# Filler products in TensorE's pauses, small products placed between weight blocks, and VectorE's norm chains through PSUM banks

## The reference, cut to what matters

```python
h = rms_norm(x, g);  z = h @ w_in                       # state-space branch, 8 heads, gates
x = x + rms_norm(merged @ w_mix_out, g)                 # norms 0 to 2
h = rms_norm(x, g)                                      # norm 3
x = x + rms_norm(cross_attention(h, mem) @ w_xo, g)     # norm 4
h = rms_norm(x, g)                                      # norm 5
x = x + rms_norm(square(relu(h @ w_ff1)) @ w_ff2, g)    # norm 6
for layer in (0, 1):                                    # norms 7 and 8
    h = rmsnorm(x, g);  z = h @ w_in_2[layer]
    x = x + mix(attention, pooling, convolution, ...) @ w_out_2[layer]
return rmsnorm(x, final_g)                              # norm 9

def rms_norm(x, g):
    return x * rsqrt(mean(x * x, -1) + EPS) * g
```

## Time and profile before

| | us |
|---|---|
| three runs | 2260.95, 2265.91, 2262.15; median 2262.15 |
| the profiled execution | 2263.18, its span 2261.5 |
| PE busy | 2159.8 (96%) |
| DVE busy | 1129.1 (50%) |
| ACT busy | 1005.3 (44%) |
| POOL busy | 795.6 (35%) |
| mean granted clock of PE | 0.979 |

### The profile page before, as it was taken

One profiled execution on the slowest core, in us unless ns is written; L12 is line 12 of the kernel. 1 busy time (PEld: TensorE's weight loads), 2 busy tenths in 40 slices (PEclk: granted clock), 3 DMA queues, 4 the chain that ended last, 5 costly groups with the idle time before them and its releaser, 6 DMA issues.

```text
span 2261.5 us, 31039 instructions
## 1 busy us (share of the span) xinstructions
PE 2159.8 (96%) x11196; PEld 1773.6 (78%) x11196; DVE 1129.1 (50%) x2003; ACT 1005.3 (44%) x1950; POOL 795.6 (35%) x347
## 2 busy tenths in 40 slices
PE   5999999999988989999999999999999999999998
PEld 4788888788887878888877877877777777877776
DVE  5799999555451447353336432222376622222374
ACT  5768786752343433222223334444633333444631
POOL 2511111444463124444442323233343333333342
PEclk9999999999999999999998999999999999999998
DMA  3212121322342122232322212222223221222221
GB/s 144 86 57 68 58 66 65 134 90 93 98 135 84 38 66 93 93 103 93 96 100 89 89 62 74 66 75 66 84 93 116 90 79 66 66 75 66 80 94 60
DMA packets 51732, 189.32 MB, mean 84 GB/s; under 512 B 6564, under 2 KB 7204, under 8 KB 51108
## 3 DMA queue, kind: packets, MB, share of 16 engines
q1 hardware_dynamic: 48096, 175.13, 24.0%
q10 hardware_dynamic: 2452, 6.88, 0.8%
q0 software_dynamic: 1072, 5.77, 0.7%
HBM read 185.66 MB, written 2.10 MB: 83 GB/s over the span
## 4 chain that ended last, share of the span: by engine, by line
PE 77%; DVE 10%; ACT 4%; issue 3%; DVEq 3%; POOL 2%; DMA 0%; ACTq 0%; POOLq 0%
PE bank L350 21%; PE bank L352 20%; PE bank L351 20%; PE bank L936 2%; PE bank L979 2%; POOL weight_lo L382 1%; PE bank L962 1%; DVE wide_region L2246 1%; ACT weight_hi L376 1%; ACT wide_region L1062 1%; DVE wide_region L2249 1%; PE bank L425 1%; PE bank L604 1%; PE bank L637 1%; PE bank L902 1%
## 5 line engine op out<-in xcount | busy, mean ns | idle before, releaser
L382 POOL TENSOR_TENSOR weight_lo<-weight_slots,weight_hi 128x1024 fp32r<-128x1024 f32 x277 | 677.5, 2446 | 1039.0 <-ACT weight_hi L376 1033.5
L376 ACT ACTIVATE weight_hi<-weight_slots 128x1024 fp32r<-128x1024 f32 x272 | 288.0, 1059 | 791.7 <-PE bank L352 706.1
L350 PE MATMUL bank<-h_hi,weight_hi 128*128 128x512 f32 x1144 | 463.6, 405 | 4.3 <-issue 3.0
L351 PE MATMUL bank<-h_lo,weight_hi 128*128 128x512 f32 x1144 | 449.1, 393 | 0.0
L352 PE MATMUL bank<-h_hi,weight_lo 128*128 128x512 f32 x1136 | 446.0, 393 | 0.0
L350 PEld LDWEIGHTS bank<-h_hi,weight_hi 128*128 128x128 f32 x1144 | 216.7, 189 | 52.3 <-issue 4.7
L352 PEld LDWEIGHTS bank<-h_hi,weight_lo 128*128 128x128 f32 x1136 | 215.0, 189 | 46.2
L351 PEld LDWEIGHTS bank<-h_lo,weight_hi 128*128 128x128 f32 x1144 | 217.2, 190 | 40.9
L382 POOL TENSOR_TENSOR head_weight_lo<-weight_slots,head_weight_hi 128x1024 fp32r<-128x1024 f32 x28 | 67.1, 2399 | 282.7 <-DVE v_region L1710 133.1
L350 PE MATMUL bank<-h_hi,head_weight_hi 128*128 128x512 f32 x336 | 139.9, 416 | 5.3 <-DVE h_lo L399 2.8
L2215 DVE RECIPROCAL small<-small 128x1 f32<-128x1 f32 x128 | 20.5, 160 | 226.5 <-ACT attention_work L1503 226.5
(11 more groups left out here) (489 smaller groups left out, 4472.2 us busy)
## 6 DMA issues: line engine op xcount, KB each, us to landing
weight_slots<-weights SPq DMA_DIRECT2D x328, 512.0 KB, 3.5
wide_region<-cmp_w ACTq DMA_DIRECT2D x2, 2048.0 KB, 9.1
v_region<-ssm_bc POOLq DMA_DIRECT2D x8, 256.0 KB, 4.6
residual<-x_in POOLq DMA_DIRECT2D x1, 2048.0 KB, 8.8
out<-normed SPq DMA_DIRECT2D x4, 512.0 KB, 2.7
residual<-x_in SPq DMA_DIRECT2D x2, 512.0 KB, 5.2
residual<-x_in ACTq DMA_DIRECT2D x2, 512.0 KB, 9.8
v_region<-mem_in POOLq DMA_DIRECT2D x1, 1024.0 KB, 5.2
```

What stands on the lines that cost most here:

```text
L350: pe.matmul(to, w_h[:, k, :], hi[:, k, 0:width], start=(k == 0), stop=False)
L351: pe.matmul(to, w_h[:, k, :], lo[:, k, 0:width], start=False, stop=False)
L376: act.activation(parts[0][s % 2], slot[s], ACT.Copy).then_inc(w_hi[s], 1)
L382: eng.tensor_tensor(parts[1][at], slot[s], parts[0][at].bitcast(F32), ALU.subtract).then_inc(w_lo[s], 1)
```

## The change

It puts idle products (a 128x128 identity by 128x512 of the mask table; nothing reads the result) at seven places of PE's order; each overwrites a bank that no one holds. It moves three groups of small products between the blocks of q0 + 4, and ACT's part of them with them. The products y * gain * root of the residual passes and of the splits go to PSUM banks (4 and 5, or 4 and 6) in place of SBUF; the split runs one block ahead in place of two and has a drain in each turn; ACT rounds from the bank. The root's correction is rewritten so that it reads the sum in bank 6 and keeps its intermediate there, with the same number of operations.

```diff
-            v, r0, rt = VAR[:, 0:tiles], R0[:, 0:tiles], RT[:, 0:tiles]
+            v, r0, rt = VAR[:, 0:tiles], R0[:, 0:tiles], bank[6][:, 16:16 + tiles]
...
-            dve.tensor_tensor(rt, r0, r0, ALU.mult)
+            dve.scalar_tensor_tensor(rt, bank[6][:, 0:tiles], D * EPS, r0, ALU.add, ALU.mult)
             dve.drain()
-            dve.scalar_tensor_tensor(rt, rt, -0.5, v, ALU.mult, ALU.mult)
+            dve.scalar_tensor_tensor(rt, rt, -0.5 / D, r0, ALU.mult, ALU.mult)
...
+        def idle_products(pe, n, to):
+
+            for _ in range(n):
+                pe.matmul(bank[to][:, :], IDENT_S, MASKS[:, 0:T], start=True, stop=True)
...
+        def split_bank(k):
+            return bank[4 + 2 * (k % 2)][:, :]
+
+        def norm_split_in_banks(dve, n, stage, hi, lo, src, gain):
 
             dve.wait_ge(bc_ready, n + 1)
             for k in range(KT + 1):
                 if k < KT:
-                    op = dve.scalar_tensor_tensor(y[:, k, :], y[:, k, :], gain[:, k:k + 1], bank[7][:, :],
+                    dve.scalar_tensor_tensor(split_bank(k), src[:, k, :], gain[:, k:k + 1], bank[7][:, :],
+                                             ALU.mult, ALU.mult).then_inc(t_ready, 1)
+                if k:
+                    rest_lo(dve, stage, k - 1, lo[:, k - 1, :], split_bank(k - 1), hi[:, k - 1, :])
+                    dve.drain()
+            dve.sem_inc(bc_used, 1)
+
+        def residual_add(dve, n, y, gain):
...
+                    op = dve.scalar_tensor_tensor(bank[4 + k % 2][:, :], y[:, k, :], gain[:, k:k + 1], bank[7][:, :],
                                                   ALU.mult, ALU.mult)
...
-                    dve.tensor_tensor(X[:, k - 1, :], X[:, k - 1, :], y[:, k - 1, :], ALU.add).then_inc(x_ready, 1)
+                    dve.tensor_tensor(X[:, k - 1, :], X[:, k - 1, :], bank[4 + (k - 1) % 2][:, :],
+                                      ALU.add).then_inc(x_ready, 1)
...
             pe.wait_ge(u_ready, KT)
+            pe.wait_ge(masks_ready, 1)
             s5_turn(0)
+            idle_products(pe, 12, 5)
             da_score(0, 0)
...
             norm_sums(pe, 4, 5)
+            idle_products(pe, 12, 3)
             norm_spread(pe, 4)
+            idle_products(pe, 18, 3)
...
             norm_sums(pe, 6, 6)
+            idle_products(pe, 8, 3)
             norm_spread(pe, 6)
+            idle_products(pe, 18, 3)
...
                     scaled_terms(3, k)
+                if L:
+                    idle_products(pe, 9, 5)
                 pe.wait_ge(evac_done[0], q0 + 1)
...
-                for s in range(4):
-                    gemm(pe, q0 + 4, s, H_HI, H_LO)
+                gemm(pe, q0 + 4, 0, H_HI, H_LO)
                 pe.wait_ge(hid_ready, L + 1)
...
+                gemm(pe, q0 + 4, 1, H_HI, H_LO)
                 pe.wait_ge(kcr_ready, L + 1)
...
+                gemm(pe, q0 + 4, 2, H_HI, H_LO)
                 pe.wait_ge(pooled_ready, L + 1)
...
+                gemm(pe, q0 + 4, 3, H_HI, H_LO)
                 pe.wait_ge(nq_ready, L + 1)
...
             norm_sums(pe, 9, 8)
+            idle_products(pe, 8, 3)
             norm_spread(pe, 9)
...
-                        round_hi(act, S_HX, k, HX_HI[:, k, :], HX[:, k, :])
+                        round_hi(act, S_HX, k, HX_HI[:, k, :], split_bank(k))
...
-                    round_hi(act, stages + S_H, k, H_HI[:, k, :], H[:, k, :])
+                    round_hi(act, stages + S_H, k, H_HI[:, k, :], split_bank(k))
...
+                store(q0 + 4, 0, RB[:, 4, :])
                 act.wait_ge(kv2_mm, L + 1)
...
+                store(q0 + 4, 1, RB[:, 5, :])
                 act.wait_ge(kc_sum, L + 1)
...
+                store(q0 + 4, 2, RB[:, 6, :])
                 act.wait_ge(pool_mm, L + 1)
...
+                store(q0 + 4, 3, RB[:, 7, :])
```

More of the change, by code:

```diff
@@ L226, in build @@
         YB = RB[:, 0:8, :]
-        HX, QX = RB[:, 8:16, :], RB[:, 24:32, :]
+        QX = RB[:, 24:32, :]
         YF = U
@@ L483, in norm_split @@
             dve.sem_inc(bc_used, 1)
+        def split_bank(k):
+            return bank[4 + 2 * (k % 2)][:, :]
+        def norm_split_in_banks(dve, n, stage, hi, lo, src, gain):
+            dve.wait_ge(bc_ready, n + 1)
+            for k in range(KT + 1):
+                if k < KT:
+                    dve.scalar_tensor_tensor(split_bank(k), src[:, k, :], gain[:, k:k + 1], bank[7][:, :],
[4 more added lines that the diff above has]
+            dve.sem_inc(bc_used, 1)
         def residual_add(dve, n, y, gain):
@@ L1473, in _ @@
                 store_values(L * 3 + (KT + 1), bank[7][:, :], FV[:, 0, :])
-                for i in range(2):
-                    for s in range(4):
-                        store(q0 + (3 + i), s, RB[:, 4 * i + s, :])
-                        if i == 0 and s == 0:
-                            store_values(L * 3 + (KT + 2), bank[6][:, :], FV[:, 1, :])
-                    if i == 0:
-                        act.wait_ge(hid_mm, L + 1)
-                        for c in range(2):
-                            op = act.activation(HID[:, 32 * c:32 * c + NC], bank[6][:, NC * c:NC * c + NC], ACT.Silu,
-                                                bias=LVEC[:, L_B1 + c:L_B1 + c + 1])
-                        op.then_inc(hid_ready, 1)
+                for s in range(4):
+                    store(q0 + 3, s, RB[:, s, :])
+                    if s == 0:
+                        store_values(L * 3 + (KT + 2), bank[6][:, :], FV[:, 1, :])
+                act.wait_ge(hid_mm, L + 1)
+                for c in range(2):
+                    op = act.activation(HID[:, 32 * c:32 * c + NC], bank[6][:, NC * c:NC * c + NC], ACT.Silu,
+                                        bias=LVEC[:, L_B1 + c:L_B1 + c + 1])
+                op.then_inc(hid_ready, 1)
+                store(q0 + 4, 0, RB[:, 4, :])
                 act.wait_ge(kv2_mm, L + 1)
@@ L1939, in _ @@
             norm_root(dve, 3)
-            norm_split(dve, 3, S_HX, HX, HX_HI, HX_LO, X, vec(V_X_PRE))
+            norm_split_in_banks(dve, 3, S_HX, HX_HI, HX_LO, X, vec(V_X_PRE))
             def xa_rest(i):
@@ L1973, in _ @@
                 if k < KT:
-                    op = dve.scalar_tensor_tensor(YB[:, k, :], YB[:, k, :], column(V_X_POST + k), bank[7][:, :],
+                    op = dve.scalar_tensor_tensor(bank[4 + k % 2][:, :], YB[:, k, :], column(V_X_POST + k), bank[7][:, :],
                                                   ALU.mult, ALU.mult)
@@ L1978, in _ @@
                 if 1 <= k <= KT:
-                    dve.tensor_tensor(X[:, k - 1, :], X[:, k - 1, :], YB[:, k - 1, :], ALU.add).then_inc(x_ready, 1)
+                    dve.tensor_tensor(X[:, k - 1, :], X[:, k - 1, :], bank[4 + (k - 1) % 2][:, :],
+                                      ALU.add).then_inc(x_ready, 1)
                 dve.drain()
@@ L2041, in _ @@
                 if k < KT:
-                    op = dve.scalar_tensor_tensor(YF[:, k, :], YF[:, k, :], column(V_FF_POST + k), bank[7][:, :],
+                    op = dve.scalar_tensor_tensor(bank[4 + k % 2][:, :], YF[:, k, :], column(V_FF_POST + k), bank[7][:, :],
                                                   ALU.mult, ALU.mult)
@@ L2046, in _ @@
                 if 1 <= k <= KT:
-                    dve.tensor_tensor(X[:, k - 1, :], X[:, k - 1, :], YF[:, k - 1, :], ALU.add).then_inc(x_ready, 1)
+                    dve.tensor_tensor(X[:, k - 1, :], X[:, k - 1, :], bank[4 + (k - 1) % 2][:, :],
+                                      ALU.add).then_inc(x_ready, 1)
                 dve.drain()
@@ L2069, in _ @@
                     scaled_out(1)
-                norm_split(dve, L + 7, stages + S_H, H, H_HI, H_LO, X, LVEC[:, L_NORM:L_NORM + KT])
+                norm_split_in_banks(dve, L + 7, stages + S_H, H_HI, H_LO, X, LVEC[:, L_NORM:L_NORM + KT])
                 for s in range(2 if L == 0 else 0, 4):
```

## The result

| | before | changed |
|---|---|---|
| median of four runs each, taken in turns on one chip | 2261.55 us | 2236.79 us |
| lowest to highest | 2260.34 to 2265.91 | 2233.67 to 2237.55 |
| the profiled execution (its span) | 2263.18 (2261.5) | 2237.55 (2234.1) |
| mean granted clock | 0.979 | 0.994 |

The ratio is 0.9884, with a 95% interval from 0.9867 to 0.9902: 25 us less. The forecast was 2236.3, in a range from 2229 to 2249. In the profiled execution of the changed kernel 3.4 us of the time lie outside the span, where they were 1.7 before; its time is 25.6 us less, its span 27.4.

What follows compares the result with a forecast made beforehand. TensorE, busy 96% of the span, was taken as the bound, partly at half clock. Terms 2.3 + 2.3 + 5.0 + 2.7 - 0.7 + 14.3 = 25.9 us gave 2237.3 from 2263.18, 2236.3 against the median; range 2229 to 2249.

Steps and rivals of the forecast that it cites:

- Small products: After the fourth block in both layers: placed between blocks, 3.95 us of waiting and 3.2 of half clock saved per layer, 14.3.
- Start of the heads: Twelve idle products in PE's 3.29 us wait for k_lo keep full clock: 2.3 us saved; 1.8 lost if the fall meets them.
- Norm 4: Before the feed-forward: 12 and 18 idle products in two waits keep spread and first products at full clock, 2.3 us saved.
- Norm 6: Before the layers: 6.3 us from full clock, less 1.3 for eight idle products running late at half clock, 5.0 us saved.
- Layer 1's pause: Before the first block of h: nine idle products in a 3.03 us wait for POOL's weight_lo, 2.7 us saved.
- Banks: Splits through two banks: longer pairs and one block less lead lose 0.7 us net; bank writes taken to cost the same as SBUF.
- rival 3: Dearer bank writes: 24 scalings and twelve operations ahead of the first lo, 0.25 us each, partly hidden; 2242 us, chance 0.11.
- Norm 9: Last norm: spread 1.0 us shorter, or idle products meet the fall and run 1.4 too long for their wait; taken as 0.
- Other falls: Five half-clock stretches of 3.4 us in pauses left unfilled, each worth 1.6, may come or go: 0, 3 to 4 us either way.
- Rival 2: Idle products, mostly zeros, do not hold the clock anywhere: only 4.9 us saved, 2257 us, chance 0.06.
- Rival 1: At norms 6 and 4 the clock falls ahead of the idle products, making them late; heads' gain lost too: 2248 us, chance 0.17.
- Rival 4: Idle products run at half clock in all seven places, small products save only waits, bank writes at upper bound: 2277 us, chance 0.04.

## Why the prediction was right

The mechanisms of the two large parts are shown: the small products by the version that has only these, the fillers by the version without any. That the sum meets the median to 0.5 us is in part luck: the terms of single falls are those of one execution, one of them has a wrong cause, and in the profiled execution the pieces give 27.1 us against 25.9. The forecast's "some 85 us" at half clock before are 93 in the span; no term rests on it.

**Small products, 14.3 forecast.** Right, and the part that is certain: 7.0 us in each layer in all eleven runs. It is 0.15 less than the forecast, and no wait is left between the blocks: ACT's wait for kc_sum ahead of its rounding held up no weight. What was called waiting was not all waiting. Of the 6.74 us before, the rows show PE idle for 1.36 and 1.56, 2.9 in all and not 3.95. The other microsecond is the clock again: L916's four products took 2.82 us, part of them at half clock, and take 1.88 now. So the clock is worth, by an estimate from these rows, about 4.1 of the 7.0, and "at worst 7.9" was too high a floor.

**Start of the heads, 2.3 forecast.** Right in the changed kernel's first profile (2.1); over all profiles, with against without, it is 0.3 to 2.6. In six of the eight profiles that have the twelve as in the change the piece is 375.3 to 375.6 us; in the other two, the changed kernel's second and that of three more pauses filled, it is 376.5, since the fall came under the fillers, the loss that the step named as its bound. The three profiles without them have 376.9 to 377.9.

**Norm 4, 2.3 forecast.** Right as a difference of two executions (2.2), too small as a price: without fillers the piece took 39.99, 42.77 and 40.91 us, with them 37.8 every time.

**Norm 6, 5.0 forecast.** Right to 0.1 in the first profile, by the step's own reason: the eight ran at half clock and late (the fall came 0.6 us after they had begun, not 0.3 ahead of them), and the clock was back for the 18. That this profile had the fall there is luck: the piece is 36.40 to 39.97 us without fillers, 31.7 in five of the profiles with them and 32.9 or 33.0 in three, so against the one profile before the gain is 6.3 in five of eight, which the step gave as its bound.

**Layer 1's pause, 2.7 forecast.** The difference is there (2.3 with the split's 0.4), its cause as stated is not: "2.7 saved" was put to the nine fillers, but two kernels without them have no fall at this place, and the piece is 34.92 us without them and 34.9 to 35.0 with them: no run shows that they save anything. The step took a fall of one execution as one that every execution has.

**Banks, -0.7 forecast.** Right in sign and size for the splits: +0.5, +0.4 and -0.4, so 0.5 lost. A scaling into a bank takes a mean of 751 to 755 ns, against 738 to 748 into SBUF, and rival 3 falls. By the Trainium skill (Perfetto Trace Analysis, Optimizing Scalar/DVE Operations) a bank should be dearer than SBUF by some 65 ns an access. The trace doesn't agree: it shows 16 ns or less for a write, and for a read 684 or 685 ns against some 680 for a rest from SBUF with POOL idle. In the kernel before, DVE's groups had

```profile
L399 DVE TENSOR_TENSOR h_lo<-normed,h_hi 128x512 fp32r<-128x512 f32 x16 | 14.5, 928 | 1.6 <-ACT h_hi L395 1.6
L399 DVE TENSOR_TENSOR hx_lo<-wide_region,hx_hi 128x512 fp32r<-128x512 f32 x8 | 6.5, 831 | 3.0 <-ACT hx_hi L395 3.0
L490 DVE SCALAR_TENSOR_TENSOR wide_region<-wide_region,vectors,bank 128x512 f32<-128x512 f32 x8 | 6.0, 748 | 13.4 <-PE bank L470 12.7
```

928 and 831 ns for rests with both operands in SBUF, and 748 for a scaling that reads a bank. Only three of these 24 rests were stretched, to 1.89, 2.54 and 2.81 us, and they are the three that ran beside POOL's weight_lo for over 0.2 us. In the changed kernel five rests of the splits and six sums of norm 2's residual pass run beside POOL, and none takes over 0.70 us: the stretching is gone with the second SBUF operand. That agrees with the Trainium skill (SBUF — State Buffer, Who interferes with whom), by which a VectorE operation with at most one SBUF input, outside the modes that use both ports, does not contend with GpSimd.

**Norm 9, 0 forecast.** Right as a middle value: 0.9 gained in the four profiles in which the clock holds, 0.0 to 0.3 lost in the five others. It is either the one or the other.

**Other falls, 0 with 3 to 4 either way.** Right, and it is likely to be most of the run-to-run spread. In the first profile they gave 1.6 twice and took 0.9 and 1.6; the 1.2 us between norms 1 and 2 turns up in four profiles of kernels with no bank in that code too and is missing in a fifth, so it is no sure part of the change.

**The rivals.** Rival 2 (the fillers don't hold the clock) is out by 11.6 us. Rival 1 is a matter of chance at each place, not a case of its own: the fall sometimes comes under the fillers at the heads, at norm 6 and at norm 9, and never did at norm 4. The sign named for being wrong, filler rows 0.43 us apart in more than one place, was all but there in the first profile: most of the eight at norm 6, and the last of the eight at norm 9. Rival 4 would have needed all of them at once.

**What stays open.** What decides in which execution a short pause lowers the clock stays open. The runs show that the same kernel has the fall in one execution and not in the next; that a shift of 1.4 us moves it is not shown, since the fall goes without a shift too. Whether the version with all gaps filled would gain by the banks too wasn't tried.

## What to carry to other kernels

Small products that depend on each other through other engines belong between blocks of independent work: that gain came whole, in every run, and needs no luck. A filled pause holds the clock more surely when the short gaps just ahead of it are filled as well: norm 4, which has none ahead, held in every profile, the heads in six of eight. Fill all of them, count the fillers so that they end half a microsecond ahead of the operand, and judge by the granted clock of the whole execution, since with only some pauses filled the clock can fall at others. And don't price a fall by one profile: profile the same kernel again, and see whether the fall stays.

## What the runs showed that was not expected

- Without fillers the half-clock stretch at norm 4 was 10.2, 13.6 or 17.1 us long, and its piece took between 39.99 and 42.77 us. The shortest and the longest are of the same code there.
- A fall comes also where no single gap is long: at 1178.3 us after one idle gap of 0.66 us, with two groups of one-column sums (0.95 and 1.05 us) on its two sides and eight idle products already running.
- The first operation of the root's correction takes a mean of 170 ns on the bank instead of 381: of its ten, of four columns or two, one had taken 2.34 us, at norm 3 from 669.9, while POOL's weight_lo ran from 669.82 for 2.39 us; the nine others took 0.16. In the changed kernel it takes 0.17 beside the same weight_lo. So a small operation is stretched as the large ones are. It saved PE nothing: norm 3's spread comes 8.73 or 8.74 us behind its sums in every version.
- Half clock costs nothing where PE waits for DVE: norm 3's split takes 56.65 us with a stretch of 3.4 us at half clock in it (no banks) and 56.7 without (gaps ahead filled).
